# A smaller ring for split feed-forward operands, and GpSimd's feature sums moved ahead of its weight sums

## The chip, the cores and the metric

The kernel runs on one core of one Trainium2 chip. The metric is device time in microseconds (us) of one execution; the median of three runs is given. Lower is better. PE is TensorE, DVE is VectorE, ACT is ScalarE, POOL is GpSimd, SP is SyncE, whose queue issues every DMA of this kernel.

## The reference, cut to what matters

The program is one layer of a transformer-like trunk on a sequence of 1024 rows of 1024 features: an attention mixer, a gated feed-forward block with a causal depthwise convolution, and a gate with a second input. All is float32. The change touches the feed-forward block and what follows it:

```python
h  = h + concat(oA, oB) @ w_out
hn = RMSNorm(h)
a, g = hn @ w_ffn_in[:, :2816], hn @ w_ffn_in[:, 2816:]
u  = gelu(causal_dwconv(a)) * g            # 1024 x 2816
h  = h + u @ w_ffn_out                     # 2816 x 1024
h  = h + sigmoid(RMSNorm(h) @ Wg) * (p @ Wp)
out = RMSNorm_final(h)
```

## The kernel before, in words

**Split products.** Float32 accuracy comes from splitting each operand into a high part (rounded to the type that TensorE multiplies) and a low part (the rest), and adding three products: high by high, high by low, low by high. The high part is made by ACT (`copy`, L787), the low part by DVE (`low`, L1195), in that order, one 128x512 tile each.

**Seven products for eight.** Both feed-forward products use a Strassen-like scheme: sums and differences of quarter blocks are multiplied, 7 products in place of 8.

**First stage, the input product.** For each of 22 feature tiles f there are seven products, numbered 1, 2, 6, 7, 5, 4, 3 in the order of the list `order` (for f 0 and 1 the order is slightly different). Each is 12 matmuls of 128x512. 154 such products make the list; a place in it is a position. The operand of each product is a slice of the weights or a sum of slices: the sums s1 and s3 are made by POOL (L718, L715), s2 and s4 by DVE (L1420). What the products give is added up by DVE (c11, u2, u3, u4, c22, c21, c12), then convolved (`tap0` on ACT, `taps` on DVE), put through gelu (ACT, `gelu`) and multiplied (`gated`, DVE, L1583) into the tile u. Of every two tiles u, POOL makes four more sums in `su` (one for an even f, three for an odd f), and SP stores seven blocks (`store_u`) to memory.

**Second stage, the output product.** Seven rounds r of 11 steps q, 77 steps s = 11 r + q. A step reads two split operands, one from the stored sums of u (loaded by `load_u` into `raw`) and one from the weights (`res`), and runs 12 matmuls. After each round DVE adds its result into h (`h_adds`, L1647), spread over the first steps of the next round; the eight adds of round 5 all stand at step (6, 0), which is step 66. `w_sums` makes sums of weight blocks on DVE. Near the end of the stage the next block is prepared: `ple_norm` (a square on ACT, a power on POOL, L1656 on DVE) and `ple_turn` (transposes on PE, ahead of steps 70 and 74).

**The ring.** Split operands of both stages live in a ring of buffers, RING = 9. Operand k goes to buffer k % 9. It may be written when the product or step that used operand k - 9 is done:

```python
def user(k):
    return k if k < NPROD else NPROD + (k - NPROD) // 2
def fills_after(pos):
    return [k for k in range(RING, NFILL) if user(k - RING) == pos]
```

ACT and DVE are in-order queues, written out by hand. After each position both have the call `fill(n, f)` (second stage: a loop over `fills_after(NPROD + s)`), which waits for that product or step and then makes the operands whose buffer it freed. Around these calls stand the other works of the queue. PE waits, ahead of a product or step, until the low parts of its operands are made (`S.op_lo`). The first nine operands are made before there is anything to wait for, by `op_hi(0)` to `op_hi(8)` and the same `op_lo` calls.

**GpSimd's queue.** After the first three tiles it runs a loop over f: `s1(f + 3)`, `s3(f + 3)`, `su(f)`. `s1(f)` waits until DVE has split operand (5, f - 1), because there is one buffer for the sum; `s3(f)` waits for (7, f - 1); `su(f)` waits until DVE has made tile u of f.

**SyncE's queue.** `load_u(s)` waits until the low part of the operand of step s - 4 has been made (four buffers in `raw`). Between these loads stand the loads of the weights (`load_b`), of h (`load_h`), and the stores of the last pair of tiles.

Of the kernel before, what the change touches and what calls it, by code (L numbers as in the profile page):

```python
# [21 lines left out]
D = 1024  # L22
# [41 lines left out]
def build(nc, x, p, w_in, w_out, sinks, lambda_q, lambda_k, subln_gain, rel_bias, norm_mix, norm_ffn,  # L64
# [7 lines left out]
    def sb(stack, name, shape, dt=F32):  # L72
        return stack.enter_context(nc.sbuf_tensor(name, shape, dt))
# [66 lines left out]
    wbuf = sb(late, "wbuf", [P, 16 * D], F32R)  # L140
# [4 lines left out]
    more = sb(late, "more", [P, 2 * D + HALF], F32R)  # L145
# [21 lines left out]

    HALF_X = slice(0, HALF), slice(HALF, SEQ)
    t4x = wbuf[:, 6 * D:10 * D].rearrange("p (j n) -> p j n", j=4)
    RING = 9  # L170
    ring_at = [more[:, 0:D], more[:, D:2 * D]] + [wbuf[:, i * D:(i + 1) * D] for i in (0, 1, 2, 3, 4, 5, 15)]

    def op(k):
        return ring_at[k % RING].rearrange("p (l n) -> p l n", l=2)

# [4 lines left out]
    def w_half(f, gate, half):  # L180
        return w_tile(f, gate)[:, HALF_X[half]]

    def w_there(eng, f, gate):

        s = 2 * (f % 2) + gate
        eng.wait_ge(raw_loaded[s] if s < 3 else S.gffn_in, (48, 48, 32, 16)[s] + 16 * (f // 2 + 1))

    def blk_there(eng, q, n):

        eng.wait_ge(wv_loaded[q], (16 if q < 5 else 0) + 16 * n)  # L190

    def s_tmp(n, f):
        if f == 0 and n <= 2:
            return gel[:, HALF_X[n - 1]]
        return xs[:, (n - 1) // 2, HALF_X[(n - 1) % 2]]

    def u_buf(f):
        return wbuf_f[:, (10 + f % 2) * D:(11 + f % 2) * D]

    def su_buf(n):  # L200
        return wbuf_f[:, 12 * D + HALF * (n - 1):12 * D + HALF * n]
# [15 lines left out]
# [6 lines that stand above are left out]
# [26 lines left out]
    def u_raw(s):  # L249
        return raw[:, s % 4 // 2, HALF_X[s % 2]]  # L250
# [428 lines left out]
    def _(pool):  # L679
# [6 lines left out]
        def power(src, dst, ready, done, n):  # L686
            pool.wait_ge(ready, n + 1)
            nc.gpsimd.tensor_tensor(dst, src, stat[:, 63:64], ALU.pow).then_inc(done, 1)  # L688
# [25 lines left out]
        def minus(dst, a, b, done):  # L714
            nc.gpsimd.tensor_tensor(dst, a, b, ALU.subtract).then_inc(done, 1)  # L715

        def plus(dst, a, b, done):
            nc.gpsimd.tensor_tensor(dst, a, b, ALU.add).then_inc(done, 1)  # L718

        def s1(f):  # L720
            w_there(pool, f, 1)
            if f == 0:
                pool.wait_ge(S.oproj, 1)
            if f == 1:
                pool.wait_ge(S.tr1, turn_no(2, 3))
            if f >= 2:
                pool.wait_ge(S.op_lo, nth[5, f - 1] + 1)
            plus(s_tmp(1, f), w_half(f, 1, 0), w_half(f, 1, 1), S.s1)

        def s3(f):  # L730
            w_there(pool, f, 0)
            if f == 0:
                pool.wait_ge(S.tr1, turn_no(2, 3))
            else:
                pool.wait_ge(S.op_lo, nth[7, f - 1] + 1)
            minus(s_tmp(3, f), w_half(f, 0, 0), w_half(f, 1, 0), S.s3)
# [12 lines left out]
        def su(f):  # L749
            q = f // 2  # L750
            pool.wait_ge(S.u_ready, f + 1)
            a0, a1 = u_buf(2 * q), u_buf(2 * q + 1)
            if f % 2 == 0:
                if q >= 1:
                    pool.wait_ge(S.u_st, 112 * q)
                minus(su_buf(3), a0[:, 0:HALF], a0[:, HALF:SEQ], S.su)
                return
            if q >= 1:
                pool.wait_ge(S.u_st, 112 * q)
            plus(su_buf(1), a0[:, HALF:SEQ], a1[:, HALF:SEQ], S.su)  # L760
            if q >= 1:
                pool.wait_ge(S.u_st, 112 * q)
            pool.wait_ge(S.su, 4 * q + 2)
            minus(su_buf(2), su_buf(1), a0[:, 0:HALF], S.su)
            if q >= 1:
                pool.wait_ge(S.u_st, 112 * q)
            pool.wait_ge(S.su, 4 * q + 3)
            minus(su_buf(4), a1[:, 0:HALF], su_buf(2), S.su)

        for f in range(NF):  # L770
            if f + 3 < NF:
                s1(f + 3)
                s3(f + 3)
            su(f)
        power(stat[:, 20:21], stat[:, 28:29], S.ms2, S.pow2, 0)
        power(stat[:, 21:22], stat[:, 29:30], S.ms2, S.pow2, 1)
        for t in range(NT + 1):
# [7 lines left out]
    def _(act):  # L785
        def copy(dst, src, done, scale=1.0):
            nc.scalar.activation(dst, src, ACT.Copy, scale=scale).then_inc(done, 1)  # L787
# [172 lines left out]
        def op_hi(k):  # L960
            if k < 2:
                act.wait_ge(S.oproj, 1)
            elif k < 4:
                act.wait_ge(S.o_row, 1)
            elif k < RING:
                act.wait_ge(S.oproj, NT)
            else:
                act.wait_ge(S.prod, user(k - RING) + 1)
            if k < NPROD:
                n, f = order[k]  # L970
                if n in (1, 2):
                    w_there(act, f, 0)
                    src = w_half(f, 0, n - 1)
                elif n == 4:
                    w_there(act, f, 1)
                    src = w_half(f, 1, 1)
                elif n == 5:
                    act.wait_ge(S.s1, f + 1)
                    src = s_tmp(1, f)
                elif n == 6:  # L980
                    act.wait_ge(S.s2, f + 1)
                    src = s_tmp(2, f)
                elif n == 7:
                    act.wait_ge(S.s3, f + 1)
                    src = s_tmp(3, f)
                else:
                    act.wait_ge(S.s4, f + 1)
                    src = s_tmp(4, f)
            else:
                s = (k - NPROD) // 2  # L990
                r, q = s // NQ, s % NQ
                if k % 2 == NPROD % 2:
                    act.wait_ge(x_loaded[s % 4], (64 if s % 4 < 2 else 0) + 16 * (s // 4 + 1))
                    src = u_raw(s)
                else:
                    if r == 0:
                        blk_there(act, q, 1)
                    elif r == 1:
                        blk_there(act, q, 2)
                    elif r == 2:  # L1000
                        blk_there(act, q, 4)
                    else:
                        act.wait_ge(S.t_low, {3: 2 * q + 2, 4: 2 * q + 1, 5: 2 * NQ + q + 1, 6: 3 * NQ + q + 1}[r])
                    src = res[B_RES[r]][q]
            copy(op(k)[:, 0, :], src, S.op_hi)
# [79 lines left out]
        x_hi(2, 3)  # L1085
        op_hi(5)
        x_hi(4, 3)
        op_hi(6)
        op_hi(7)
        op_hi(8)  # L1090
        for n, f in order[0:4]:
            fill(n, f)
        fill(6, 0)
# [91 lines left out]
    def _(dve):  # L1185
# [7 lines left out]
        def low(dst, src, hi, done, scale=None):  # L1193
            if scale is None:
                ins = nc.vector.tensor_tensor(dst, src, hi.bitcast(F32), ALU.subtract)  # L1195
            else:
                ins = nc.vector.scalar_tensor_tensor(out=dst, in0=src, scalar=scale, in1=hi.bitcast(F32),  # L1197
                                                     op0=ALU.mult, op1=ALU.subtract)
            if done is not None:
                ins.then_inc(done, 1)  # L1200
            return ins
# [220 lines left out]
        def s2(f):  # L1422
            dve.wait_ge(S.s1, f + 1)
            w_there(dve, f, 0)
            minus(s_tmp(2, f), s_tmp(1, f), w_half(f, 0, 0)).then_inc(S.s2, 1)

        def s4(f):
            if f == 0:
                dve.wait_ge(S.tr1, turn_no(2, 3))
            dve.wait_ge(S.s2, f + 1)  # L1430
            minus(s_tmp(4, f), w_half(f, 0, 1), s_tmp(2, f)).then_inc(S.s4, 1)

        def op_lo(k):
            if k < NPROD:
                n, f = order[k]
                if n == 6:
                    s2(f)
                    if f >= 1:
                        s4(f)
                if (n, f) == (7, 0):  # L1440
                    s4(0)
                src = (w_half(f, 0, n - 1) if n in (1, 2) else w_half(f, 1, 1) if n == 4
                       else s_tmp({5: 1, 6: 2, 7: 3, 3: 4}[n], f))
            else:
                s = (k - NPROD) // 2
                src = u_raw(s) if k % 2 == NPROD % 2 else res[B_RES[s // NQ]][s % NQ]
            dve.wait_ge(S.op_hi, k + 1)
            low(op(k)[:, 1, :], src, op(k)[:, 0, :], S.op_lo)
# [143 lines left out]
        x_lo(2, 3)  # L1592
        op_lo(5)
        x_lo(4, 3)
        op_lo(6)
        op_lo(7)
        op_lo(8)
        for n, f in order[0:4]:
            fill(n, f)
        u2(0)  # L1600
# [624 lines left out]
```

## Time and profile before

| | |
|---|---|
| median of 3 runs | 1224.47 us (1223.74 to 1225.08) |
| the profiled execution | 1223.96 us |
| its span, first to last instruction | 1222.0 us |
| PE busy | 1188.1 us, 97% |
| DVE busy | 867.0 us, 71% |
| ACT busy | 521.7 us, 43% |
| POOL busy | 243.2 us, 20% |
| mean granted TensorE clock | 0.996 of full |

The profiled execution is 0.51 us under the median of the runs, and its span 1.96 us under its own time. A time read from the trace is counted from the first instruction. Busy times of different engines overlap, so a share of busy time says only how much room an engine has on average, not where it is late.

### The profile page before, as it was taken

The page shows a single profiled execution, that of the slowest core. Times are in us where ns is not written, and L with a number is a line of the kernel's source. Part 1 is how long each engine was busy: PE and PEld are TensorE (multiplying, and loading weights), DVE is VectorE, ACT ScalarE, POOL GpSimd, SP SyncE. Part 2 cuts the span into 40 slices and gives each one's busy share as a digit, 9 for nine tenths or more (in the row PEclk, how much of TensorE's full clock was granted, in tenths as well). Part 3 has the DMA queues.
Part 4 walks back from the last instruction along what each step waited for, and adds up shares of the span by engine and source line. Part 5 has one row for each costly group of instructions (what it writes and reads, how often), then busy time and mean ns, then how long its engine had stood idle before and what let it go on. Part 6 is the DMA issues. An engine that isn't in the chain of part 4 may idle for free.

```text
span 1222.0 us, 17029 instructions
## 1 busy us (share of the span) xinstructions
PE 1188.1 (97%) x6119; PEld 992.3 (81%) x6119; DVE 867.0 (71%) x1522; ACT 521.7 (43%) x1053; POOL 243.2 (20%) x287
## 2 busy tenths in 40 slices
PE   8999999999898999999999999999999999999997
PEld 7997887887676787888888888888888888888886
DVE  5423786777887569977788777787778899864443
ACT  4321665665655335433333333343344444643321
POOL 0000000354455002232331333313210000000000
PEclk9999999999999999999999999999999999999999
DMA  8464233111832413233333333333498533620101
GB/s 225 89 89 89 52 88 86 31 42 67 226 137 54 154 52 103 81 110 112 104 104 94 105 112 104 109 95 99 155 365 305 158 101 108 221 69 26 43 35 52
DMA packets 127916, 136.08 MB, mean 111 GB/s; under 512 B 15714, under 2 KB 93274, under 8 KB 127770
## 3 DMA queue, kind: packets, MB, share of 16 engines
q1 hardware_dynamic: 127834, 135.00, 36.6%
q8 instruction: 49, 0.80, 0.3%
q14 instruction: 33, 0.27, 0.1%
HBM read 96.77 MB, written 37.22 MB: 110 GB/s over the span
## 4 chain that ended last, share of the span: by engine, by line
PE 65%; issue 1%; DMA 1%; DVE 1%; ACT 0%; DVEq 0%; POOLq 0%; POOL 0%; ACTq 0%
PE ps L1757 64%; PE ps L1763 1%; DMA raw<-in_w_out 1%; DVE wbuf L1195 0%; PE ps L2135 0%; DVE a_t L1195 0%; DVE h L1722 0%; DVE conv L1719 0%; ACT conv L790 0%; ACT wbuf L787 0%; PE ps L1949 0%; ACT a_t L787 0%; DVE e_t L1309 0%; DVE gel L1750 0%; DVE h L1337 0%
## 5 line engine op out<-in xcount | busy, mean ns | idle before, releaser
L1757 PE MATMUL ps<-act_t,wbuf 128*128 128x512 f32 x1200 | 280.1, 389 | 0.0
L1757 PEld LDWEIGHTS ps<-act_t,wbuf 128*128 128x128 f32 x1200 | 225.1, 188 | 47.0 <-DVE a_buf L1529 0.3
L1757 PE MATMUL ps<-wbuf 128*128 128x512 f32 x912 | 214.8, 390 | 0.0
L1757 PEld LDWEIGHTS ps<-wbuf 128*128 128x128 f32 x912 | 170.6, 188 | 35.1
L1757 PE MATMUL ps<-act_t,wq 128*128 128x512 f32 x624 | 152.2, 396 | 3.7 <-DVE wq L1197 3.0
L1757 PEld LDWEIGHTS ps<-act_t,wq 128*128 128x128 f32 x624 | 114.2, 188 | 30.9 <-issue 7.5
L787 ACT ACTIVATE wbuf<-raw 128x512 fp32r<-128x512 f32 (+1 forms) x107 | 69.2, 648 | 77.4 <-PE ps L1757 62.9
L688 POOL TENSOR_TENSOR stat<-stat 128x1 f32<-128x1 f32 x32 | 17.6, 550 | 423.1 <-DVE stat L1204 423.1
L1195 DVE TENSOR_TENSOR wbuf<-raw,wbuf 128x512 fp32r<-128x512 f32 (+1 forms) x107 | 87.8, 820 | 14.7 <-ACT wbuf L787 14.2
L1757 PE MATMUL ps<-hx,wbuf 128*128 128x512 f32 x408 | 95.7, 389 | 1.4 <-issue 1.4
L1757 PEld LDWEIGHTS ps<-hx,wbuf 128*128 128x128 f32 x408 | 76.5, 188 | 17.7 <-issue 1.8
L869 ACT ACTIVATE e_t<-ps,small 128x128 f32<-128x128 f32 (+7 forms) x64 | 47.4, 742 | 63.4 <-DVE small L1324 62.3
L787 ACT ACTIVATE wbuf<-xs 128x512 fp32r<-128x512 f32 x66 | 39.9, 625 | 70.9 <-DVE xs L1420 54.2
L1757 PE MATMUL ps<-wbuf,act_t 128*128 128x512 f32 x288 | 68.2, 393 | 0.2 <-DVE wbuf L1195 0.2
L1757 PEld LDWEIGHTS ps<-wbuf,act_t 128*128 128x128 f32 x288 | 53.2, 188 | 11.3 <-DVE wbuf L1195 0.6
L1757 PE MATMUL ps<-wq,act_t 128*128 128x384 f32 (+1 forms) x384 | 58.1, 310 | 1.5 <-DVE wq L1195 1.4
L1757 PEld LDWEIGHTS ps<-wq,act_t 128*128 128x128 f32 x384 | 56.5, 188 | 1.9 <-issue 1.6
L1757 PE MATMUL ps<-act_t,more 128*128 128x512 f32 x240 | 56.9, 389 | 0.0
L715 POOL TENSOR_TENSOR wbuf_f<-wbuf_f 128x512 f32<-128x512 f32 x33 | 52.2, 1581 | 18.6 <-DVE wbuf_f L1583 15.6
L1195 DVE TENSOR_TENSOR a_t<-ps,a_t 128x512 fp32r<-128x512 f32 (+4 forms) x64 | 44.6, 715 | 14.5 <-ACT a_t L787 14.4
L1757 PEld LDWEIGHTS ps<-act_t,more 128*128 128x128 f32 x240 | 45.0, 188 | 9.4
L1195 DVE TENSOR_TENSOR wbuf<-xs,wbuf 128x512 fp32r<-128x512 f32 x66 | 50.3, 763 | 0.5
(202 smaller groups left out, 1942.3 us busy)
## 6 DMA issues: line engine op xcount, KB each, us to landing
u_ops<-wbuf_f SPq DMA_DIRECT2D x77, 256.0 KB, 2.3
raw<-u_ops SPq DMA_DIRECT2D x77, 256.0 KB, 2.8
raw<-in_w_ffn_in SPq DMA_DIRECT2D x33, 512.0 KB, 3.8
g_ffn<-in_w_ffn_in SPq DMA_DIRECT2D x11, 512.0 KB, 4.0
act_f<-in_w_ffn_out SPq DMA_DIRECT2D x21, 256.0 KB, 3.8
w_raw<-in_w_in SPq DMA_DIRECT2D x10, 512.0 KB, 4.2
wbuf_f<-in_w_ffn_out SPq DMA_DIRECT2D x18, 256.0 KB, 6.5
x_in<-in_x SPq DMA_DIRECT2D x8, 512.0 KB, 3.7
```

The costliest lines, as they stand in the source:

```text
L688: nc.gpsimd.tensor_tensor(dst, src, stat[:, 63:64], ALU.pow).then_inc(done, 1)
L715: nc.gpsimd.tensor_tensor(dst, a, b, ALU.subtract).then_inc(done, 1)
L787: nc.scalar.activation(dst, src, ACT.Copy, scale=scale).then_inc(done, 1)
L869: nc.scalar.activation(e_t[:, pr, m, 0:w], psf[:, at:at + w], ACT.Exp, scale=-1.0, bias=small[:, o + 2 + m:o + 3 + m], accum_out=small[:, ...
L1195: ins = nc.vector.tensor_tensor(dst, src, hi.bitcast(F32), ALU.subtract)
L1757: return nc.tensor.matmul(dst, lhs, rhs, start=start, stop=stop)
L1763: ins = nc.tensor.transpose(psf[:, bank * HALF + k * P:bank * HALF + (k + 1) * P], src[:, k * P:(k + 1) * P], ident[:, :])
```

## The change

Three edits. The ring gets six buffers: the last three, in `wbuf` at places 4, 5 and 15, are no longer used. Operands 6, 7 and 8 are no longer made ahead of the first fills, but by them. And in GpSimd's loop `su(f)` comes first, ahead of `s1(f + 3)` and `s3(f + 3)`. All code that depends on RING follows, so in every queue the operand made after a position is three places nearer to its use.

```diff
-    RING = 9
-    ring_at = [more[:, 0:D], more[:, D:2 * D]] + [wbuf[:, i * D:(i + 1) * D] for i in (0, 1, 2, 3, 4, 5, 15)]
+    RING = 6
+    ring_at = [more[:, 0:D], more[:, D:2 * D]] + [wbuf[:, i * D:(i + 1) * D] for i in (0, 1, 2, 3)]
...
         for f in range(NF):
+            su(f)
             if f + 3 < NF:
                 s1(f + 3)
                 s3(f + 3)
-            su(f)
...
         op_hi(5)
         x_hi(4, 3)
-        op_hi(6)
-        op_hi(7)
-        op_hi(8)
         for n, f in order[0:4]:
             fill(n, f)
...
         op_lo(5)
         x_lo(4, 3)
-        op_lo(6)
-        op_lo(7)
-        op_lo(8)
         for n, f in order[0:4]:
             fill(n, f)
```

## Rows read from the trace of the kernel before

**Rows 1.** The page's busy times: us, share of the span, instructions.
```profile
PE 1188.1 (97%) x6119; PEld 992.3 (81%) x6119; DVE 867.0 (71%) x1522; ACT 521.7 (43%) x1053; POOL 243.2 (20%) x287
```

**Rows 2.** The chain that ended last: start us, us, what.
```profile
477.34 1.43 issue
478.77 598.67 PE ps L1757 x2640
```

**Rows 3.** Timeline of PE: start us, us, instructions; idle before in brackets.
```profile
886.88 2.88 PE L1757 MATMUL ps<-wbuf,more 128*128 128x512 f32 x12
...
1077.28 0.38 PE L2135 MATMUL ps<-ident,xs 128*128 128x128 f32 x2
```

**Rows 4.** Timeline of DVE, first stage, around its latest split.
```profile
643.53 0.69 DVE L1562 TENSOR_TENSOR wbuf_f<-ps,more_f 128x512 f32<-128x512 f32 x1 [3.97 <-DMA u_ops<-wbuf_f]
...
650.71 0.69 DVE L1195 TENSOR_TENSOR more<-xs,more 128x512 fp32r<-128x512 f32 x1
```

**Rows 5.** Waits from 478 to 887 us: who waited for whom, total, times, longest.
```profile
DVE wbuf_f L1562 <- DMA u_ops<-wbuf_f: 36.3, 10, 4.0
```

**Rows 6.** Timeline of DVE, start of the second stage.
```profile
892.99 1.28 DVE L1577 SCALAR_TENSOR_TENSOR conv<-a_buf,cols,conv 128x1024 f32<-128x1024 f32 x1
...
896.53 0.68 DVE L1195 TENSOR_TENSOR wbuf<-raw,wbuf 128x512 fp32r<-128x512 f32 x1
897.13 1.22 DVE L1583 TENSOR_TENSOR wbuf_f<-wbuf_f,gel 128x1024 f32<-128x1024 f32 x1
...
898.87 1.78 DVE L1195 TENSOR_TENSOR wbuf<-raw,wbuf 128x512 fp32r<-128x512 f32 x1
900.58 1.78 DVE L1195 TENSOR_TENSOR wbuf<-act_f,wbuf 128x512 fp32r<-128x512 f32 x1
902.28 1.77 DVE L1195 TENSOR_TENSOR wbuf<-raw,wbuf 128x512 fp32r<-128x512 f32 x1
...
904.58 0.68 DVE L1195 TENSOR_TENSOR more<-raw,more 128x512 fp32r<-128x512 f32 x1
```

**Rows 7.** Timeline of POOL in the same stretch.
```profile
898.43 1.67 POOL L718 TENSOR_TENSOR wbuf_f<-wbuf_f 128x512 f32<-128x512 f32 x1 [14.83 <-DVE wbuf_f L1583]
900.25 3.26 POOL L715 TENSOR_TENSOR wbuf_f<-wbuf_f 128x512 f32<-128x512 f32 x2
```

**Rows 8.** Timeline of DVE around step 66.
```profile
1070.48 4.87 DVE L1647 TENSOR_TENSOR h<-ps,h 128x512 f32<-128x512 f32 x8
1075.27 0.69 DVE L1195 TENSOR_TENSOR wbuf<-wbuf_f,wbuf 128x512 fp32r<-128x512 f32 x1
1075.87 0.69 DVE L1195 TENSOR_TENSOR wbuf<-raw,wbuf 128x512 fp32r<-128x512 f32 x1
```

**Rows 9.** The chain that ended last, where PE had waited for DVE.
```profile
403.69 1.24 DVE wbuf L1195
...
404.97 8.46 PE ps L1757 x36
```

**Rows 10.** Timeline of SP's DMA queue, from the load for step 8 to that for 14.
```profile
888.76 0.38 SPq L589 DMA_DIRECT2D raw<-u_ops  x1
...
910.11 0.68 SPq L589 DMA_DIRECT2D raw<-u_ops  x1
```

**Rows 11.** Timeline of ACT, the split of the block loaded for step 14.
```profile
919.57 0.63 ACT L787 ACTIVATE wbuf<-raw 128x512 fp32r<-128x512 f32 x1 [4.66 <-DMA raw<-u_ops]
```

**Rows 12.** Busy time by stretch: PE, PEld, DVE, ACT, POOL, granted clock, DMA share, GB/s.
```profile
315.70:319.10 3.40, 3.11 (x17) 2.74 (x17) 3.29 (x9) 2.97 (x10) 0.92 (x3) 0.50 1.03 229
...
910.00:914.00 4.00, 4.00 (x19) 3.34 (x18) 1.78 (x4) 1.90 (x3) 0.00 (x0) 1.00 1.05 404
```

**Rows 13.** Timeline of PE at idle times of over 1.5 us.
```profile
315.43 0.30 PE L1932 MATMUL ps<-ident,bias_a 128*128 128x128 f32 x1 [1.62 <-POOL bias_a L713]
...
384.43 1.06 PE L1949 MATMUL ps<-ident,e_t 128*128 128x128 f32 x8 [2.05 <-DVE act_t L1195]
```

## The prediction

> **What bounds the kernel now.** The page's busy times come first: PE is busy for 97% of the span, DVE for 71%, POOL for 20% [rows 1]. The chain of waits then says where that matters: from 478.77 to 1077.44 us it is one unbroken run of 2640 matmuls, with no other engine in it [rows 2]. That run is both feed-forward stages from product (6, 0) on. The only idle time near it is the 1.43 us ahead of it. So until 1077 us PE never waits for an operand, and the change can save nothing inside the run. It can only add, where an operand now comes too late. The question is how late each split is against its new due time.
>
> The timeline of PE gives the clock for that. Step 0 begins at 886.88 and step 70's transposes at 1077.28 [rows 3]: 70 steps in 190.40 us, 2.72 us for 12 matmuls. Step s ends at 886.88 + 2.72 (s + 1), and a position of the first stage is as long.
>
> **The ring, first stage.** With nine buffers an operand made after position i is used at i + 9; with six, at i + 6, that is five products, 13.6 us, after i has ended. The count of splits after each position stays one, so ACT's and DVE's queues keep their order and nearly their times; only the names move by three. I read the end of the low part after every position. The latest follows position 63, product (1, 9), which ends at 886.88 - 90 x 2.72 = 642.08: the low part ends at 650.71 + 0.69 = 651.40 [rows 4], 9.3 us later. Room left: 13.6 - 9.3 = 4.3 us. That lateness comes from a wait of 3.97 us for the stores of u [rows 4], one of ten such waits with 36.3 us in all [rows 5]. Cost: 0, hidden by that room; if DVE came over 4.3 us later still, each further us would be paid once per pair of tiles.
>
> **Operands 6 to 8** are made by the first fills instead, whose products have ended by then; DVE makes them in the same order behind `x_lo(4, 3)`. The idle 1.43 us ends when an earlier instruction of DVE's queue (`x_lo(3, 3)`) does, so it stays. Cost: 0.
>
> **GpSimd's order.** With six buffers operand (5, f + 2), for which `s1(f + 3)` waits, is made after product (4, f + 1), three products (8.2 us) later than before. `su(f)` needs only the tile u, ready after (6, f + 1). Put first, it doesn't stand behind the later wait, and even the two sums that it used to follow are out of its way (in a like stretch POOL needs 1.6 to 1.7 us for one [rows 7]). The stores follow su, so DVE's ten waits for them should shrink by up to some 3 us each. PE waits in none of them: gain 0. `s1` and `s3` in turn are needed by DVE after (7, f + 2), four products after their trigger, 10.9 us for two instructions. On SP, `load_a(f)` waits for s4, now three products later, and the store of a pair stands behind it; it still comes before su is done, since su waits for `gated` and then works some 5 us. The weight tile itself has over ten products until its use. Cost: 0. The last three turns of the loop have no s1 or s3, so the last `su(21)` starts as before.
>
> **The ring, second stage.** Here a step uses two operands. Nine buffers: after step s one operand of step s + 4 and one of s + 5 are made. Six: both of step s + 3, due when step s + 2 ends, 5.44 us after the release. Again two splits stand at each place, so DVE's times stay and I compare them with the new due time. Of 72 steps the second low part is later than 5.44 us, for work of the queue itself, in two stretches (in a third, steps 9 to 11, at most 6.8 us, and there for a load that is no longer due then; below).
>
> *Steps 2 and 3.* Behind step 0 DVE runs `taps(21)` to 894.27, ACT a gelu, then come two splits, `gated` for 1.22 us and four more splits, three of which take 1.78 us instead of 0.68 [rows 6]. They overlap with POOL's three sums of `su(21)`, 898.43 to 903.51 [rows 7]. Step 1's fill: 896.53 + 0.68 = 897.21, due 897.76: in time by 0.55. Step 2's: 900.65, due 900.48. Step 3's: 904.05, due 903.20. PE starts 0.04 us after the end of the DVE instruction it waits for (403.69 + 1.24, against 404.97 [rows 9]). So step 5 starts 0.21 late and step 6 at 904.09, 0.89 late in all; the first is contained in the second. Step 7's pair ends at 905.26 [rows 6], due 905.92: in time.
>
> Why those splits are slow decides this stall. The rows show DVE at 1.7 us a split exactly while POOL sums: each ends some 0.55 us after a sum of POOL. At the 0.60 us a split of the others, step 3's pair would end near 900.7, and no stall would be left: the sum would be lower by 0.9 and one restart, 2.2 in place of 3.3. The Trainium skill, "SBUF — State Buffer", section "Who interferes with whom", says that a DVE instruction with two SBUF inputs and a GpSimd one that reads SBUF exclude each other, and who issues first holds the port for the whole instruction. By that rule, the trace agrees; and by it a split that got in ahead of a sum would be short and the stall smaller.
>
> *Step 66.* DVE ends `ple_norm(0)`, adds eight times for 4.87 us, and then splits: the second low part ends at 1076.56 [rows 8]. Step 66 ended at 1069.12, so it is 7.44 us late. Now it belongs to step 69, due at 1074.56. PE waits until 1076.56 + 0.04: 2.04 us. The earlier stall moves PE and this queue alike, so it takes nothing off. Step 70 is then later too and its operands (1077.8) are in time, with transposes ahead of it. The steps after 69 have 1 us of room or more; everywhere else in the stage it is 0.5 us or more.
>
> *Restart.* After a wait PE's next 36 matmuls took 8.46 us, where 36 of the run take 8.16: 0.3 lost [rows 9]. After the idle time at 477 us the 150 products to 886.88 took 408.11, against 408.0 [rows 2, 3]: 0.1. I take 0.2, in the middle, for each of the two stalls; ends 0.1 and 0.3.
>
> **Sum.** 0.89 + 2.04 + 2 x 0.2 = 3.3 us; with the ends 3.1 to 3.5, and some tenths either way for modelled ends: 2.9 to 3.9. Behind step 76 all follows PE, so nothing is given back. Profiled execution 1223.96 + 3.3 = 1227.3; the median of the runs stands 0.51 above it, so 1227.8, own range 1227.3 to 1228.4.
>
> **Rivals.**
>
> *No loss.* DVE finds room that I don't see: its splits interleave otherwise with POOL, and at step 66 the order of waits lets a pair in sooner. Against it: the queue is written out, and the eight adds stand ahead of the split. 1224.5. If only the first stall fails to come: 1224.47 + 2.2 = 1226.7.
>
> *The burst of loads.* The load for step 8 waits for a low part that now ends at 896.60, so it moves from 888.76 [rows 10] by 7.9 us. From it to the load for step 14 SP issues 9.17 MB by the sizes in the code; at 404 GB/s [rows 12] that is 22.7 us, and the block for step 14 lands at 919.5 [rows 11]. New: 896.7 + 22.7 and some 1.5 for the loads just ahead of it, about 921. It must be there by 923.5 (step 14 is due at 925.9, less 2.4 us for the splits). Hidden by 2.5 us. Were the whole 7.9 us added, to 927.4, it would cost 3.9 more: 1231.7.
>
> *The clock.* A stall of 2 us could drop TensorE to the lower of its two levels, 1.2 GHz. The rows have it at 0.50 for 3.4 us, from 315.7, just as PE had stood idle for 1.62 us; but it stayed at full after an idle time of 2.05 us at 384.43 [rows 12, 13]. Price: half of 3.4, 1.7 us: 1229.5.
>
> *The first stage.* If DVE's lateness grows past the 4.3 us of room, PE stalls in each pair of tiles; at 1 us over, once in each of ten pairs, 10 us: 1234.5.
>
> *Faster.* The sums of su come earlier and DVE waits less. This ends in a gain only if DVE's queue holds PE, and the whole of PE's idle time that could be won around the run is 1.43 us: 1223.0, within what can't be told from no change.
>
> **How the numbers follow.** Both stalls 0.60; only the second 0.09; no loss 0.13; the burst 0.07; the clock 0.06; the first stage 0.03; faster 0.02. The time is that of the likeliest. A measurement of this kernel can tell about 0.2%, 2.45 us, from no change, so the bound is 1226.9. Slower than it: the likeliest case but for 0.06 of it, in which the sum comes out too high (0.54), the burst, the clock and the first stage: 0.70. Within: 0.06, 0.09, 0.13: 0.28. Faster by more: 0.02, at most. The range from 1225.2 to 1230.0 leaves out no loss, faster, the first stage and a part of the burst, 0.20.
>
> **What would show it.** PE's timeline: unbroken from 478.8 to about 900, up to 0.9 us of idle time ahead of steps 5 and 6, released by DVE's low split, unbroken again, and one of about 2 us ahead of step 69, released by the split behind the eight adds. DVE's rows keep their times to 1075. The ten waits for the stores shrink with nothing gained. The prediction is wrong if PE idles in the first stage, if a load releases it near step 14, if the clock falls near 1077, or if the pair for step 69 is made before the adds.

## The result: 1231.97 us, 0.5% slower than before, and the profile after

The kernel after the change takes 1231.97 us (median of 4 runs, 1230.67 to 1234.59), against 1224.78 us (4 runs, 1223.74 to 1225.17): ratio 1.0053, interval 1.0034 to 1.0073. The forecast was 1227.8 with a range to 1230.0: right in sign, but 7.2 us were lost where 3.3 were expected. The profiled execution took 1234.59 us, the longest of the four; its span is 1232.7 us. All executions that are compared here and below are in the chip's faster state; one of the kernel before, of 6789.52 us beside experiments 9 to 11, is left out.

The page's busy times. DVE has 34.5 us more than in [rows 1] for the same 1522 instructions, POOL 3.5 us more:

```profile
PE 1193.2 (97%) x6119; PEld 995.6 (81%) x6119; DVE 901.5 (73%) x1522; ACT 518.3 (42%) x1053; POOL 246.7 (20%) x287
```

Timeline of PE: the first row is the start of the run, which stood at 478.77 in [rows 2]. All rows with idle time from there to the transposes are shown, and the first rows of steps 0, 5 and 7:

```profile
482.40 5.72 PE L1751 MATMUL ps<-hx,wbuf 128*128 128x512 f32 x24 [1.43 <-issue]
...
844.67 2.98 PE L1751 MATMUL ps<-act_t,wbuf 128*128 128x512 f32 x12 [0.23 <-DVE wbuf L1192]
...
850.80 3.00 PE L1751 MATMUL ps<-act_t,more 128*128 128x512 f32 x12 [0.43 <-DVE more L1192]
...
891.72 1.52 PE L1751 MATMUL ps<-wbuf 128*128 128x512 f32 x6
...
905.55 3.04 PE L1751 MATMUL ps<-wbuf 128*128 128x512 f32 x12
908.95 3.02 PE L1751 MATMUL ps<-wbuf 128*128 128x512 f32 x12 [0.36 <-DVE wbuf L1192]
...
911.80 1.07 PE L1751 MATMUL ps<-more 128*128 128x512 f32 x4
...
931.67 5.73 PE L1751 MATMUL ps<-wbuf 128*128 128x512 f32 x24 [0.67 <-DVE wbuf L1192]
...
1083.45 4.60 PE L1751 MATMUL ps<-wbuf 128*128 128x512 f32 x12 [1.89 <-DVE wbuf L1192]
1087.90 0.38 PE L2129 MATMUL ps<-ident,xs 128*128 128x128 f32 x2
```

From the start of the run to the first transposes it is 1087.90 - 482.40 = 605.50 us, against 1077.28 - 478.77 = 598.51: 6.99 us. I call this length R and use it below, since it leaves out what varies ahead of the run; it is always that of the profiled execution. It splits thus, against the same stretches in [rows 2, 3]:

| stretch | after | before | lost |
|---|---|---|---|
| first stage, to step 0 | 409.32 | 408.11 | 1.21 |
| steps 0 to 6 | 20.08 | 19.04 | 1.04 |
| steps 7 to 13 | 19.87 | 19.04 | 0.83 |
| steps 14 to 68, with the wait of 69 | 151.78 | 149.60 | 2.18 |
| step 69's own matmuls | 4.45 | 2.72 | 1.73 |

The second and the fourth row are the two stalls of the forecast, which gave 0.89 + 0.2 and 2.04 + 0.2. The other three rows, 3.77 us, are not in its sum. Each is one of its rivals (first stage, burst of loads, clock), and all three came at once.

The idle time in brackets is less than what is lost, because twelve matmuls take 2.88 us by their row and 2.72 us from start to start. Step 5 starts at 905.55, which is 0.23 us late and prints no idle time; step 6 starts at 908.95, 0.91 us late, and prints 0.36; behind it another 0.13 us go. The forecast had 0.21, 0.89 and 0.2.

**The first stage.** The chain of waits shows what made the product at 850.80 late. It runs from DVE's sum s4 over SP's queue and a store back to DVE:

```profile
831.91 1.68 DVE xs L1417
833.61 0.37 SPq L539
...
834.07 0.53 SPq L558
...
837.67 5.44 DMA u_ops<-wbuf_f
...
843.23 0.12 DVE wbuf_f L1559
...
846.50 2.25 DVE conv L1572
...
850.80 43.81 PE ps L1751 x192
```

`load_a` (L539) waits for s4; the six stores of the pair (L558 and on) stand behind it in SP's queue; c21 (L1559) overwrites what the last of them reads. Waits from 478 to 892 us:

```profile
DVE wbuf_f L1559 <- DMA u_ops<-wbuf_f: 45.5, 9, 6.1
```

and of SP's queue in the same stretch:

```profile
SPq L539 <- DVE xs L1417: 181.2, 20, 11.3
...
SPq L567 <- POOL wbuf_f L715: 1.4, 1, 1.4
```

The same view of the kernel before:

```profile
SPq L539 <- DVE xs L1420: 164.7, 20, 9.5
...
SPq L563 <- POOL wbuf_f L718: 31.8, 10, 3.7
...
SPq L567 <- POOL wbuf_f L715: 13.8, 10, 1.5
```

So before, the stores themselves waited for POOL's sums; now the sums are there when `load_a` is released, and `load_a` alone holds the stores. The waits for stores, 36.3 us in [rows 5], grew instead of shrinking. At the same time DVE's own instructions are longer. The timeline of POOL and then that of DVE beside it:

```profile
820.64 1.29 POOL L718 TENSOR_TENSOR xs<-g_ffn 128x512 f32<-128x512 f32 x1 [5.14 <-DVE wbuf L1192]
821.89 1.75 POOL L715 TENSOR_TENSOR xs<-raw,g_ffn 128x512 f32<-128x512 f32 x1
```

```profile
821.02 1.46 DVE L1192 TENSOR_TENSOR wbuf<-raw,wbuf 128x512 fp32r<-128x512 f32 x1
822.42 2.30 DVE L1572 SCALAR_TENSOR_TENSOR conv<-a_buf,cols,conv 128x1024 f32<-128x1024 f32 x1
824.75 1.28 DVE L1574 SCALAR_TENSOR_TENSOR conv<-a_buf,cols,conv 128x1024 f32<-128x1024 f32 x1
```

The sums s1 and s3 now start when DVE splits (5, f + 2) and (7, f + 2), three products later than before. There DVE has a split and the taps in hand: 1.46 and 2.30 us beside POOL, where the next taps, alone, take 1.28. DVE's groups by shape from 540 to 800 us (us busy, mean ns of one, idle before) say that the taps are so on the mean of 13 tiles. The sums s4, 692 ns before, are longer too; the one at 831.91 lies beside POOL's feature sums, not beside s1 and s3:

```profile
L1572 DVE SCALAR_TENSOR_TENSOR conv<-a_buf,cols,conv 128x1024 f32<-128x1024 f32 x13 | 29.3, 2257 | 0.5 <-ACT conv L1071 0.5
...
L1417 DVE TENSOR_TENSOR xs<-raw,xs 128x512 f32<-128x512 f32 x14 | 16.5, 1182 | 0.5
```

In the kernel before, the same taps take 1285 ns and have 17.2 us of idle time ahead of them. The next group is that of the kernel before, same view:

```profile
L1575 DVE SCALAR_TENSOR_TENSOR conv<-a_buf,cols,conv 128x1024 f32<-128x1024 f32 x14 | 18.0, 1285 | 17.2 <-ACT conv L1071 17.2
```

c21 of an even tile shows the period of this loop. Timeline of DVE, the first and the ninth that wait for a store:

```profile
532.89 0.69 DVE L1559 TENSOR_TENSOR wbuf_f<-ps,more_f 128x512 f32<-128x512 f32 x1 [4.84 <-DMA u_ops<-wbuf_f]
...
843.23 0.69 DVE L1559 TENSOR_TENSOR wbuf_f<-ps,more_f 128x512 f32<-128x512 f32 x1 [6.15 <-DMA u_ops<-wbuf_f]
```

That is 310.34 / 8 = 38.79 us for a pair of tiles, where PE needs 14 x 2.72 = 38.08. DVE falls behind by 0.7 us per pair on the mean, and in the ninth the room is used up. It does so unevenly: by 0.3 to 0.6 us in six of the eight intervals, by 1.1 in the third and 1.8 in the last, where the wait for the store is 6.15 us. In experiment 9, the same kernel again, that wait is 4.84 us and no stall follows. What makes a single store 1.3 us longer is not shown.

**Step 14.** Timeline of ACT at the split of its block, and of SP's queue at the load of it:

```profile
929.66 0.63 ACT L787 ACTIVATE wbuf<-raw 128x512 fp32r<-128x512 f32 x1 [5.62 <-DMA raw<-u_ops]
```

```profile
919.18 0.49 SPq L589 DMA_DIRECT2D raw<-u_ops  x1
```

Against step 0, the block's split stood 919.57 - 886.88 = 32.69 us behind it before [rows 3, 11] and stands 37.94 behind it now: 5.25 us later, while step 14 itself is due 1.04 us later by the stall at step 6. Of the 5.25, the issue of the load gives 4.23 (27.46 us behind step 0 against 23.23) and its landing 1.0. The forecast had it land at about 921, some 1.5 us later than before. Its way there, from the issue of the load for step 8 to this landing, has the following busy times and rate (columns as in [rows 12]):

```profile
901.48:929.60 28.12, 27.69 (x121) 22.29 (x120) 17.49 (x22) 10.04 (x18) 4.78 (x3) 1.00 1.02 386
```

The load for step 8 was issued as forecast, 9.76 us behind step 0 (901.48 - 891.72) where 896.7 - 886.88 = 9.82 was expected. Then 28.1 us passed where the forecast had 22.7 + 1.5 = 24.2. In them 386 GB/s moved 10.9 MB; the forecast had 9.17 MB and 1.5 us more at 404 GB/s, 9.8 MB. The lower rate accounts for some 1.2 us and the further 1.1 MB for some 2.7.

**Step 69.** Timeline of DVE:

```profile
1077.33 4.87 DVE L1641 TENSOR_TENSOR h<-ps,h 128x512 f32<-128x512 f32 x8
...
1082.72 0.68 DVE L1192 TENSOR_TENSOR wbuf<-wbuf_f,wbuf 128x512 fp32r<-128x512 f32 x1
```

The split ends at 1083.40 and PE starts at 1083.45, as forecast. What was not: the 12 matmuls behind this stall took 4.60 us. The stretch's busy times and clock (columns as in [rows 12]):

```profile
1083.45:1087.90 4.45, 4.45 (x13) 3.49 (x14) 2.36 (x4) 0.00 (x0) 0.00 (x0) 0.62 0.60 175
```

### The profile page after: what moved, and what is told of

It reads as the page before. It is cut to its first block and busy times, and to the rows that moved or that the text cites. A ratio compares the mean times of both kernels' runs of the same rounds, so it can differ in the third digit from the quotient of the medians.

```text
span 1232.7 us, 17009 instructions
## 1 busy us (share of the span) xinstructions
PE 1193.2 (97%) x6119; PEld 995.6 (81%) x6119; DVE 901.5 (73%) x1522; ACT 518.3 (42%) x1053; POOL 246.7 (20%) x287
## 5 line engine op out<-in xcount | busy, mean ns | idle before, releaser
L1751 PE MATMUL ps<-act_t,wbuf 128*128 128x512 f32 x1080 | 252.5, 389 | 0.2 <-DVE wbuf L1192 0.2
L1751 PEld LDWEIGHTS ps<-act_t,wbuf 128*128 128x128 f32 x1080 | 202.5, 188 | 42.9 <-issue 0.6
L1751 PE MATMUL ps<-wbuf 128*128 128x512 f32 x864 | 206.7, 393 | 3.0 <-DVE wbuf L1192 2.9
L787 ACT ACTIVATE wbuf<-raw 128x512 fp32r<-128x512 f32 (+1 forms) x93 | 60.9, 655 | 83.2 <-PE ps L1751 70.7
L1192 DVE TENSOR_TENSOR wbuf<-raw,wbuf 128x512 fp32r<-128x512 f32 (+1 forms) x93 | 72.8, 783 | 29.6 <-ACT wbuf L787 29.4
L1751 PE MATMUL ps<-hx,wbuf 128*128 128x512 f32 x372 | 87.5, 389 | 1.4 <-issue 1.4
L1751 PE MATMUL ps<-act_t,more 128*128 128x512 f32 x360 | 85.5, 389 | 0.4 <-DVE more L1192 0.4
L1751 PEld LDWEIGHTS ps<-act_t,more 128*128 128x128 f32 x360 | 67.5, 188 | 14.8 <-issue 0.8
L1751 PE MATMUL ps<-more 128*128 128x512 f32 x312 | 75.1, 389 | 0.0
L1751 PEld LDWEIGHTS ps<-more 128*128 128x128 f32 x312 | 58.5, 188 | 12.1
```

The source lines that it names most:

```text
L1751: return nc.tensor.matmul(dst, lhs, rhs, start=start, stop=stop)
```

## Experiments

Eleven kernels ran, in three batches; medians stand beside those of the kernel before on the same chip. All compute the whole layer but the two of which it is said. The intervals of most ratios overlap that of the changed kernel (1.0034 to 1.0073), so what an edit mends is read from the idle times on PE, not from the medians. R has a part by chance too: behind step 69 the clock fell in the profiled executions of the changed kernel and of experiments 6, 9 and 11, which is 1.3 to 1.6 us of R more than behind the same wait at full clock, and not in the others. Unless a row says otherwise, the edit is made to the changed kernel. Line numbers move by a few.

**1. Ring of nine, GpSimd's new order alone.**

```diff
-    RING = 6
-    ring_at = [more[:, 0:D], more[:, D:2 * D]] + [wbuf[:, i * D:(i + 1) * D] for i in (0, 1, 2, 3)]
+    RING = 9
+    ring_at = [more[:, 0:D], more[:, D:2 * D]] + [wbuf[:, i * D:(i + 1) * D] for i in (0, 1, 2, 3, 4, 5, 15)]
...
+        op_hi(6)
+        op_hi(7)
+        op_hi(8)
...
+        op_lo(6)
+        op_lo(7)
+        op_lo(8)
```

> The kernel before with GpSimd's new order alone, nine buffers. Theory (the order costs nothing by itself): 1224.8 us within 0.5, PE unbroken from about 479 us on, and DVE's waits for the stores of u fall from 36 us to under 15. Rival (the moved sums slow DVE through their shared port and that paces the first stage): DVE busy grows from 867 towards 901 us and the time by 1 us or more.

Measured: 1225.0 us (12 runs) against 1225.04, ratio 0.9996 (0.9986 to 1.0005); R 598.53; no stall of PE. So the order by itself costs nothing, and the loss comes only with the shorter ring. It also shortens no wait for the stores. Waits from 478 to 892 us:

```profile
DVE wbuf_f L1562 <- DMA u_ops<-wbuf_f: 36.0, 10, 3.7
```

The part that I had expected to fall to under 15 us did not. The stores do end earlier: c21 of the ninth pair starts 352.02 us behind the start of the run, against 354.78 before. But DVE gets there earlier by as much, since the 12.8 us that it waited for POOL ahead of c22 from 540 to 800 us are gone. And `conv` L1575 takes 1284 ns as before and DVE's busy time is 855.3 us: with nine buffers the weight sums don't fall on the taps. The other half, six buffers with GpSimd's old order, was not tried: by the code, s1(f + 3) would wait for operand (5, f + 2), made behind c21(f + 1), which waits for stores of su(f), which stands behind that s1. The circle closes, so the reorder is a condition of the small ring, not a second idea; no run shows it.

**2. The stores ahead of `load_a`.**

```diff
         for f in range(2, NF):
-            load_a(f)
             if f >= 4:
                 store_u(f - 4)
+            load_a(f)
             load_g(f)
```

> The changed kernel with SyncE's queue storing a tile of u ahead of loading the next weight tile, so that the stores no longer stand behind the wait for the sum s4. Theory (the loop DVE s4 - SyncE load - stores - DVE c21 paces the first stage at 38.8 us a pair of tiles against TensorE's 38.1): the two stalls near 845 and 851 us vanish, DVE's waits for the stores fall from 45 us to under 20, the time falls by 1.2 to about 1230.8. Rival (DVE is slowed by its own longer instructions and has no room either way): the waits fall but the stalls stay, 1232.

Measured: 1229.35 us (10 runs), ratio 1.0029 (1.0018 to 1.0041); R 602.69. The waits for the stores from 478 to 892 us are gone, and so are the stalls of the first stage:

```profile
DVE wbuf_f L1559 <- DMA u_ops<-wbuf_f: 0.7, 2, 0.5
```

Timeline of PE, all its idle rows behind the run's start:

```profile
904.51 3.02 PE L1751 MATMUL ps<-wbuf 128*128 128x512 f32 x12 [0.34 <-DVE wbuf L1192]
...
927.22 5.73 PE L1751 MATMUL ps<-wbuf 128*128 128x512 f32 x24 [0.65 <-DVE wbuf L1192]
...
1079.00 3.02 PE L1751 MATMUL ps<-wbuf 128*128 128x512 f32 x12 [1.89 <-DVE wbuf L1192]
```

The taps L1572 are at 1285 ns again, with 32.2 us of idle time ahead of them. So SP's queue was one leg of the loop. And here step 69's matmuls took 3.02 us behind the same 1.89 us: the clock did not fall. Of the 2.8 us that R is shorter here, only 1.2 are the first stage's.

**3. The eight adds spread, two to a step.**

```diff
-                if q == 0:
-                    h_adds(5, 0, 8)
+                if q < 4:
+                    h_adds(5, 2 * q, 2 * q + 2)
```

> The changed kernel with the eight adds of round 5 spread, two at each of the steps 66 to 69, instead of all at step 66. Theory (the splits for step 69 stand behind the block of adds, and the stall of 1.9 us there also lowers TensorE's clock): no idle time ahead of step 69, no lower clock behind it, 2.2 plus up to 1.7 less: about 1228.3. Rival (the adds only move the lateness): a stall of 1 us or more ahead of one of the steps 70 to 73, and under 1 us gained.

Measured: 1230.11 us (10 runs), ratio 1.0032 (1.002 to 1.0043); R 602.38. Step 69 is in time, but the transposes ahead of step 70 wait for the last of the adds. Timeline of PE:

```profile
1080.92 0.44 PE L2129 MATMUL ps<-ident,xs 128*128 128x128 f32 x2 [1.58 <-DVE h L1641]
```

That is the rival of the expectation; the 1228.3 us of the theory were not reached. The eight adds made step 69 late, as forecast; spread, they move most of the stall (1.58 of 1.89 us) by one step.

**4. Ring of seven** (one buffer and one `op_hi(6)`, `op_lo(6)` more than the changed kernel).

```diff
-    RING = 6
-    ring_at = [more[:, 0:D], more[:, D:2 * D]] + [wbuf[:, i * D:(i + 1) * D] for i in (0, 1, 2, 3)]
+    RING = 7
+    ring_at = [more[:, 0:D], more[:, D:2 * D]] + [wbuf[:, i * D:(i + 1) * D] for i in (0, 1, 2, 3, 4)]
```

> The changed kernel with seven buffers, GpSimd's new order kept. Theory (each due time moves by a place in the first stage, and in the second one operand of each pair is due a step later): no stall in the first stage, none at steps 5 and 6, and ahead of step 69 about 1.3 us, by the first low part alone: 1226 to 1227. Rival (the depth is not what counts, but the order of the queues): 1231 to 1232.

Measured: 1227.12 us (12 runs), ratio 1.0014 (1.0003 to 1.0025); R 600.34. Timeline of PE, its one idle row:

```profile
1078.91 3.04 PE L1753 MATMUL ps<-wbuf 128*128 128x512 f32 x12 [1.29 <-DVE wbuf L1193]
```

One more buffer removes all the stalls but the one that was 2 us late.

**5. The last su over 2 columns** (leaves out nearly all of the last three feature sums).

```diff
+            w = HALF if f < NF - 1 else 2
-            plus(su_buf(1), a0[:, HALF:SEQ], a1[:, HALF:SEQ], S.su)
+            plus(su_buf(1)[:, 0:w], a0[:, HALF:HALF + w], a1[:, HALF:HALF + w], S.su)
```

(and the two `minus` in the same way)

> The changed kernel with the last three feature sums of GpSimd (tile 21) made over 2 columns instead of 512, so most of that work is left out and the blocks stored from it are not the right ones. Theory (the splits behind step 2 are late only because they wait for these sums at the shared port): three splits take 0.68 instead of 1.78 us, no idle time ahead of steps 5 and 6, about 1.0 us less than the changed kernel. Rival (the order of the queue alone makes them late): the idle 0.36 us ahead of step 6 stays, under 0.3 us gained.

Measured: 1231.67 us (5 runs), ratio 1.0056 (1.0043 to 1.0069); R 602.76. DVE's splits of steps 2 and 3 take 0.68 us and step 6 is in time: the overlap with POOL was the cause of the first stall, as forecast. But hardly anything is won. Timeline of PE:

```profile
927.23 5.74 PE L1752 MATMUL ps<-wbuf 128*128 128x512 f32 x24 [1.75 <-DVE wbuf L1193]
```

PE reaches step 14 earlier and waits there longer; the block sets that time, not PE. Step 14 starts 448.12 us behind the start of the run, against 448.63 in experiment 9, which has no stall in the first stage either.

**6. The load of the gain vector moved from step 13 to step 34.**

```diff
             if s == 13:
                 store_u(NF - 1)
+            if s == 34:
                 sp.dma_start(g_ple[:, :], row(norm_ple, D)).then_inc(S.gple_in, 16)
```

> The changed kernel with the load of the norm's gain (512 KB) moved from between the loads for steps 13 and 14 to the load for step 34, out of the burst. Theory (ahead of step 14 TensorE waits for a block of u that lands late behind everything queued before it): the block lands some 1.3 us earlier and the idle 0.67 us ahead of step 14 is gone, about 0.8 us less than the changed kernel. Rival (the block is late because SyncE issues its load late, not because of the queue): the idle time stays within 0.2 us.

Measured: 1230.09 us (6 runs), ratio 1.004 (1.0026 to 1.0053); R 604.69. Step 14 is in time. Timeline of ACT, the split of its block:

```profile
924.01 0.63 ACT L788 ACTIVATE wbuf<-raw 128x512 fp32r<-128x512 f32 x1 [3.79 <-DMA raw<-u_ops]
```

That is 36.10 us behind step 0 (at 887.91), 1.84 earlier than in the changed kernel: the load lands in time for step 14 once one transfer ahead of it is gone. The first-stage stalls are 0.59 and 0.45 us here, and the clock fell at step 69 (12 matmuls in 4.34 us).

**7. All remedies together, with six buffers.** Edits 2, 3 and 6; `gated(21)` behind the splits of step 2; and the first transposes with their operands one step later, so that they don't wait for the adds.

```diff
-            if s == 2:
-                gated(NF - 1)
...
+            if s == 2:
+                gated(NF - 1)
...
-            if (r, q) == (6, 4):
+            if (r, q) == (6, 5):
```

(the first two in DVE's queue ahead of and behind the loop over `fills_after(NPROD + s)`; the last at its three places)

> Six buffers with four places mended: the stores ahead of the weight loads, the last product with the gelu behind the splits of its step, the gain's load out of the burst, and the eight adds spread over steps 66 to 69 with the transposes of the next block one step later. Theory (four separate late splits make up the whole loss): TensorE unbroken from 479 us to the transposes, and 1225.0 us, within 0.2% of the kernel before. Rival (six buffers leave too little room as such, and a mended place gives way to the next): at least one idle time over 0.3 us remains and the time is 1227 or more.

Measured: 1225.92 us (11 runs) against 1224.92, ratio 1.0008 (0.9998 to 1.0018): not told from no change. R is 601.47 with one step more in it, so 598.75. PE runs unbroken from 479.53 to the second transposes. Its timeline there:

```profile
1091.04 0.44 PE L2130 MATMUL ps<-ident,xs 128*128 128x128 f32 x2 [0.59 <-DVE xs L1651]
```

This wait is new: DVE makes their operand a step later as well, and the second transposes have kept their place. From the start of the run to them it is 611.51 us, against 610.52 in the kernel before, which is about the difference of the medians. So the rival has a part too: one idle time over 0.3 us remains, though the time stays under its 1227.

**8. s1 and s3 over 2 columns from f = 3 on** (leaves out nearly all of these weight sums).

```diff
+            w = HALF if f < 3 else 2
-            plus(s_tmp(1, f), w_half(f, 1, 0), w_half(f, 1, 1), S.s1)
+            plus(s_tmp(1, f)[:, 0:w], w_half(f, 1, 0)[:, 0:w], w_half(f, 1, 1)[:, 0:w], S.s1)
```

(and `minus` for s3 in the same way)

> The changed kernel with GpSimd's weight sums s1 and s3 made over 2 columns from the fourth tile on, so most of that work is left out and products 5, 6, 7 and 3 are not the right ones. Theory of contention (the later weight sums now fall on DVE's longest instructions and make its pair of tiles longer than TensorE's 38.1 us): DVE busy falls from 901 to about 850 us, DVE's taps take 1.28 again instead of 2.30, and the two stalls of the first stage vanish, 1.2 us less. Theory of the store loop alone: DVE's wait for the stores grows by what its instructions lose and the stalls near 845 us stay.

Measured: 1230.17 us (6 runs), ratio 1.0043 (1.0031 to 1.0056); R 602.80. The stalls of the first stage are gone, with SP's order unchanged. Groups of DVE from 540 to 800 us, then waits from 478 to 892 us:

```profile
L1574 DVE SCALAR_TENSOR_TENSOR conv<-a_buf,cols,conv 128x1024 f32<-128x1024 f32 x14 | 18.0, 1284 | 19.9 <-ACT conv L1073 19.9
```

```profile
DVE wbuf_f L1561 <- DMA u_ops<-wbuf_f: 45.1, 10, 5.9
```

The waits for the stores stay at 45 us, but c21 comes every (833.45 - 528.72) / 8 = 38.09 us. So the two parts of the loop are separate: either the wait or the overlap alone can be borne, both cannot. DVE is busy for 870.0 us, not the 850 that were expected: its sums s4 still take 1182 ns.

**9. The changed kernel again, unaltered.**

> The changed kernel unaltered, on one chip with the next two. Theory (four places of late splits, 5.3 us, and in some executions a lower clock behind the last): 1230 to 1232 us, the same five idle times on TensorE at the same places within 0.1 us. Rival (the first reading of 1231.97 was a chance of its chip): under 1228.

Measured: 1230.89 us (6 runs) against 1225.6, ratio 1.0042 (1.0029 to 1.0055); R 604.75. Timeline of PE, all its idle rows behind the run's start:

```profile
905.62 3.01 PE L1751 MATMUL ps<-wbuf 128*128 128x512 f32 x12 [0.36 <-DVE wbuf L1192]
...
928.93 5.73 PE L1751 MATMUL ps<-wbuf 128*128 128x512 f32 x24 [1.25 <-DVE wbuf L1192]
...
1080.71 4.54 PE L1751 MATMUL ps<-wbuf 128*128 128x512 f32 x12 [1.89 <-DVE wbuf L1192]
```

The same kernel has no stall in the first stage here and a larger one at step 14. The expected same five idle times within 0.1 us did not come. Between these two executions single stalls differ by up to 0.7 us; the sum of the idle times hardly does (3.58 and 3.50 us).

**10. Adds spread, first transposes one step later.** Edit 3 and the last edit of 7.

> The changed kernel with the eight adds spread over steps 66 to 69 and, unlike the run with the adds alone, the transposes of the next block and the splits of their result one step later. Theory (with the adds spread, TensorE waited 1.6 us ahead of the transposes for the last adds and for nothing else): no idle time over 0.3 us between steps 66 and 73, some 2.2 us less than the changed kernel, and 1.7 more in executions where that one would have dropped its clock. Rival (DVE has too much work in these steps wherever it stands): 1 us or more of idle time appears ahead of a step from 70 to 75.

Measured: 1229.42 us (9 runs), ratio 1.0033 (1.0022 to 1.0044). No idle time from step 66 to 73, and no fall of the clock; ahead of the second transposes (step 74) PE waits 0.59 us, as in experiment 7. R is 605.66 with a step more in it, so 602.94: the other stalls were large in this execution (0.48, 0.47, 0.34, 1.57 us), and cover part of the gain.

**11. `gated(21)` behind the splits, and edit 6.**

> The changed kernel with the last product with the gelu behind the splits of step 2 and the gain's load out of the burst. Theory (the first makes the splits for steps 5 and 6 timely although the sums of GpSimd stay, the second takes up what the first hands on to step 14): no idle time from step 0 to step 68, 1.9 us less than the changed kernel; the stalls of the first stage and ahead of step 69 stay. Rival (what is won at step 6 comes back at step 14, as with the small sums, where that idle time grew from 0.67 to 1.75 us): over 0.5 us of idle time ahead of step 14.

Measured: 1229.79 us (8 runs), ratio 1.0035 (1.0023 to 1.0046); R 604.09. Timeline of PE, all its idle rows behind the run's start:

```profile
842.05 2.98 PE L1752 MATMUL ps<-act_t,wbuf 128*128 128x512 f32 x12 [0.62 <-DVE wbuf L1193]
...
848.19 2.98 PE L1752 MATMUL ps<-act_t,more 128*128 128x512 f32 x12 [0.44 <-DVE more L1193]
...
1078.83 4.61 PE L1752 MATMUL ps<-wbuf 128*128 128x512 f32 x12 [1.89 <-DVE wbuf L1193]
```

With both edits the stalls of steps 6 and 14 are both gone. With step 6 alone mended (5), step 14 waits longer.

## Why the prediction was right or wrong

**Right: that nothing could be gained, and the two stalls.** PE waited at steps 6 and 69, released by the splits that were named, and 1.04 and 2.18 us were lost where 1.09 and 2.24 were forecast; step 5 too was late as forecast (0.23 us, forecast 0.21). The 2.18 hold the wait of step 69, some 2.05 us, and some 0.13 behind step 14, as much as was lost behind step 6; what step 69 lost on its restart is in the last row of the table. Each cause was removed by itself: with POOL's last sums gone the first doesn't come (experiment 5), with the adds spread the second leaves its place (3).

**Wrong: "The ring, first stage ... nearly their times ... Cost: 0".** This step failed. The order in DVE's queue stayed, but its times did not: the taps went from 1285 to 2257 ns, and a pair of tiles took DVE 38.79 us where PE needs 38.08. This cost 1.21 us in the profiled execution. Three products' delay of the trigger moved s1 and s3 of POOL onto a split and the taps. The room of 4.3 us was read about right; what was wrong is that the lateness stayed at 9.3 us. The table gives, for several executions, when c21 of the ninth pair starts, counted from the start of the run (354.78 us in the kernel before), how long it had waited for the store, and PE's idle time in the first stage:

| kernel | c21, ninth pair | its wait, us | idle, us |
|---|---|---|---|
| 2, stores first | 350.29 | - | 0 |
| 8, s1 and s3 small | 355.24 | 4.95 | 0 |
| 9, changed, again | 359.18 | 4.84 | 0 |
| 5, last su small | 359.28 | 4.80 | 0 |
| 3, adds spread | 360.13 | 5.99 | 0.25 |
| changed | 360.83 | 6.15 | 0.66 |
| 10 | 361.09 | 5.99 | 0.95 |
| 6 | 361.28 | 5.96 | 1.04 |
| 11 | 361.42 | 5.98 | 1.06 |

Lateness beyond that of before is hidden up to 4.5 us (359.28) and shows from 5.35 us (360.13) on, which brackets the room just above the 4.3 us of the forecast. The changed kernel stands on that edge, so one execution pays 1.2 us and the next nothing: wherever PE stalled, that one wait was 6 us long and not 4.8 to 5. The rival had the mechanism right (a lateness that grows), and its price wrong: 10 us would need 1 us more in every pair and no room ahead of the first; at 0.5 to 0.8 us more per pair only the ninth reaches the edge, and the tenth no longer waits for a store. Its time was also added to the kernel before, 1224.5, and not, as the other prices were, to 1227.8.

**Wrong: "GpSimd's order ... should shrink ... it still comes before su is done".** `load_a` waits 181.2 us in all for s4, 16.5 more than before, and holds the stores, whose own waits for POOL's sums fell from 56.8 to 2.8 us. The waits for the stores grew by 9.2 us; with the stores ahead of it they are 0.7 us (experiment 2). I had followed SP's queue for one tile, with DVE's times of before, and not round the loop over DVE, SP and the stores.

On the overlap itself, the forecast had looked at steps 2 and 3 alone. The Trainium skill, "SBUF — State Buffer", section "Who interferes with whom", names no stage: a DVE instruction with two SBUF inputs contends with a GpSimd one that reads SBUF. The taps here have two such inputs (`a_buf`, `conv`) and went from 1285 to 2257 ns, so the trace agrees. Applied to every sum of POOL that the change moves, it could have warned of this.

**Mis-sized: the room of the burst.** "Hidden by 2.5 us" was -0.8. The forecast added transfer times at 404 GB/s from the load for step 8 on, and got 1.5 us of delay; the block came 5.25 us later, 10.4 us after its issue. The issue of the load for step 8 was forecast right; the way from there took 28.1 us and not 24.2, with 1.1 MB more moved and at 386 GB/s. Removing the gain load ahead of it is enough to cure it (6, 11), so the transfers ahead of it hold it. Whether the further 1.1 MB stood ahead of this load or were moved beside it is open. This stall also undoes what is saved at step 6, as experiment 5 shows.

**Rival come true: the clock.** Its price, 1.7 us, was right (the stretch lost 1.73, some 0.14 of which are lost at full clock too). It was given 0.06; it fell in 4 of 7 executions with the idle time of 1.89 us, the changed kernel's two profiles among them.

**The sum of the true terms**: 1.21 + 1.04 + 0.83 + 2.18 + 1.73 = 6.99 us, R's difference, beside 7.19 us in the medians. The likeliest case let three small rivals fall, each with a chance of its own. Two of them were not independent: the places in the first stage and at step 14 lost their room by the same edit. The third, the clock, hangs on the stall that was itself forecast. Luck has a part in the size: R grew by 7.0 us where both the long store wait and the fall of the clock came, by 6.2 in experiment 9, with the fall alone, and by 4.2 in experiment 2, with neither.

**A better version?** None beats the kernel before. Its run has no idle time in it, so buffers can win nothing there; experiment 7 frees three buffers at a cost that the medians can't tell from none and that its trace puts at 1.0 us.

## What to carry to other kernels

When a ring gets shorter, each place loses room; compare not only the last instruction's end with its new due time, but also redo the times of the queues whose triggers move, above all which instructions of two engines now fall together. A loop over several queues has a period: 0.7 us more per iteration than PE's is nothing in one iteration and can be a stall after eight. And several places near their edge are not independent: mending one stall sends the work earlier into the next.

## What was not expected of the hardware

**Clock after a short idle time.** TensorE stayed at its full level (2.4 GHz) behind 2.05 us of idle time in [rows 13], but behind 1.89 us at step 69 it fell towards the lower level in 4 of 7 executions: 12 matmuls in 4.34 to 4.61 us in place of 3.02, at a mean granted clock of 0.62 to 0.67 of full from there to the transposes. In experiments 2, 5 and 8, with the same idle time, it stayed at 1.00. What decides it these runs don't show.

**GpSimd beside DVE.** Taps of 128x1024 went from 1.28 to 2.30 us beside a POOL sum, a split of 128x512 from 0.68 to 1.46 or 1.78 us. POOL's own sum of that size took 1.29 to 1.75 us.

**Landing under a burst.** A block that was issued at 919.18 us landed 10.4 us later; it had taken 9.4 us before (910.11 to 919.5, [rows 10, 11]). With the gain load gone from the queue (experiment 6) it took 9.3.
